# Joined moving operands, two-pass sums of squares for three head vectors, and a later scaling of the fox key

## The reference

```python
def hybrid_layer(h, ...):                       # first block
    u = rms_norm(h, mix_norm_g)
    p = u @ w_in                                # 2048 -> qkv_a, z, b, a, qkv_b, f, two gates
    y_a = gated_deltanet_branch(...)            # 16 heads of 128
    y_b = fox_branch(...)                       # 16 heads of 128
    mix = sigmoid(gate_a) * (y_a @ w_o_gdn) + sigmoid(gate_b) * (y_b @ w_o_fox)
    h = h + mix @ w_out
    u = rms_norm(h, mlp_norm_g)
    return h + square(relu(u @ w_up)) @ w_down

# what the change touches inside a head:
k  = k * rsqrt(sum(k * k) + eps)                # gated deltanet key, over 128
fq = fq * rsqrt(mean(fq * fq) + eps) * gain     # fox query
fk = fk * rsqrt(mean(fk * fk) + eps) * gain     # fox key
# in each chunk of 128 tokens: solve (I + strict_lower(beta k k^T decay)) w = rhs
```

## Time and profile before

| | us |
|---|---|
| median of 3 runs | 2772.41 |
| lowest and highest | 2772.25, 2773.69 |
| the profiled execution's own time | 2774.34 |
| its span | 2772.5 |
| PE busy in the span | 2740.4 (99%) |
| DVE, ACT, POOL busy | 2018.1, 1409.7, 290.1 |
| mix stage, about | 58 to 917 of the span |

### The profile page before, as it was taken

How to read it: one execution, slowest core, us unless ns; L and a number is a source line. 1 busy time by engine, 2 the same in 40 slices (tenths; PEclk the granted TensorE clock), 3 DMA queues, 4 the chain that set the end, 5 groups by cost and what they waited for, 6 DMA issues and landing times.

```text
span 2772.5 us, 50822 instructions
## 1 busy us (share of the span) xinstructions
PE 2740.4 (99%) x17645; PEld 2466.9 (89%) x17645; DVE 2018.1 (73%) x3665; ACT 1409.7 (51%) x2437; POOL 290.1 (10%) x259
## 2 busy tenths in 40 slices
PE   7999999999999999999999999999999999999998
PEld 7999999999999888888888888888888998888887
DVE  7887888788788666667765666756777777788875
ACT  6556655655665434444443444534545555445553
POOL 0000000000000000004700000000460001500024
PEclk9999999999999999999999999999999999999999
DMA  6444444444454555566565555665555554554445
GB/s 216 150 156 138 155 142 155 138 148 154 142 155 135 178 190 188 183 191 217 177 196 189 181 192 182 190 192 182 192 177 175 164 168 159 183 166 144 144 156 181
DMA packets 130235, 472.74 MB, mean 171 GB/s; under 512 B 15136, under 2 KB 15136, under 8 KB 129952
## 3 DMA queue, kind: packets, MB, share of 16 engines
q1 hardware_dynamic: 126144, 457.37, 51.3%
q0 software_dynamic: 3936, 13.34, 1.6%
HBM read 468.40 MB, written 2.25 MB: 170 GB/s over the span
## 4 chain that ended last, share of the span: by engine, by line
PE 95%; DVE 2%; ACT 1%; issue 1%; DMA 0%; DVEq 0%; SPq 0%; ACTq 0%
PE bank L310 42%; PE bank L311 21%; PE bank L312 7%; PE bank L313 7%; PE bank L314 7%; PE bank L808 1%; PE bank L854 1%; PE bank L863 1%; DVE w_lo L286 1%; PE bank L1078 1%; PE bank L1238 0%; PE bank L920 0%; PE bank L1155 0%; PE bank L1254 0%; PE bank L874 0%
## 5 line engine op out<-in xcount | busy, mean ns | idle before, releaser
L286 DVE TENSOR_TENSOR w_lo<-raw,w_hi 128x1024 fp32r<-128x1024 f32 x862 | 1058.7, 1253 | 133.5 <-ACT w_hi L280 129.2
L280 ACT ACTIVATE w_hi<-raw 128x1024 fp32r<-128x1024 f32 x862 | 896.9, 1053 | 438.6 <-PE bank L311 426.4
L310 PE MATMUL bank<-u,w_hi 128*128 128x512 f32 x2768 | 995.9, 401 | 0.0
L311 PE MATMUL bank<-u,w_lo 128*128 128x256 f32 x2768 | 779.0, 281 | 0.0
L310 PE MATMUL bank<-ya,w_hi 128*128 128x512 f32 x1792 | 629.7, 395 | 0.7 <-DVE h L2199 0.7
L310 PEld LDWEIGHTS bank<-u,w_hi 128*128 128x128 f32 x2768 | 520.5, 188 | 115.5 <-issue 2.8
L311 PEld LDWEIGHTS bank<-u,w_lo 128*128 128x128 f32 x2768 | 523.0, 189 | 0.9
L311 PE MATMUL bank<-ya,w_lo 128*128 128x256 f32 x1792 | 504.9, 282 | 0.0
L312 PE MATMUL bank<-u,w_hi 128*128 128x272 f32 (+2 forms) x1552 | 483.5, 312 | 4.9 <-DVE u L434 2.9
L313 PE MATMUL bank<-u,w_hi 128*128 128x272 f32 (+2 forms) x1552 | 445.3, 287 | 0.0
L314 PE MATMUL bank<-u,w_lo 128*128 128x272 f32 (+2 forms) x1552 | 445.1, 287 | 0.0
(11 more groups left out here) (401 smaller groups left out, 3140.3 us busy)
## 6 DMA issues: line engine op xcount, KB each, us to landing
raw<-in_stream SPq DMA_DIRECT2D x864, 512.0 KB, 3.7
mix_row<-rows POOLq DMA_DIRECT2D x16, 408.0 KB, 4.7
xT<-in_xT SPq DMA_DIRECT2D x4, 544.0 KB, 5.9
mix_coef_m<-meta_rows POOLq DMA_DIRECT2D x16, 128.0 KB, 4.5
h<-in_xT POOLq DMA_DIRECT2D x1, 2048.0 KB, 9.4
out_dram<-h SPq DMA_DIRECT2D x8, 256.0 KB, 2.4
consts<-in_consts POOLq DMA_DIRECT2D x1, 1817.0 KB, 8.2
meta_rows<-mix_b_mat POOLq DMA_DIRECT2D x16, 1.0 KB, 3.0
```

Of the source, the lines that this page charges most:

```text
L280: act.activation(w_hi[:, slot], raw[:, slot], ACT.Copy).then_inc(hi_ready, 1)
L286: dve.tensor_tensor(w_lo[:, slot], raw[:, slot], w_hi[:, slot].bitcast(F32), ALU.subtract).then_inc(lo_ready, 1)
L310: pe.matmul(o, a, x, start=first, stop=False)
L311: return pe.matmul(o[:, 0:SEQ], b, x[:, 0], start=False, stop=last)
```

## The change

Three things are changed.

The layout: `ya` becomes `[P, KT, 536]`, of which the first 512 elements are used, in one piece: part 0 and part 1 stand side by side, with 2144 bytes from one `k` to the next. A second name `ux` with the same layout is put on `u`'s place. From the MLP on, writers and readers of `u` use `ux` (up, the second block's projections and gates); the mix and merge stages still read `u` in the old layout. What lies behind `ya` moves by 512 bytes.

The sums: for the deltanet key, the fox query and the fox key, ScalarE squares twice, into a float32r tile `sq_hi` and into `sq`. VectorE writes the rest, `sq` minus `sq_hi`, over `sq` as float32r. TensorE multiplies both by float32r ones (`ones_r`), in two matmuls. The deltanet output's sum stays as it was. The new VectorE step stands at 70 (key), 90 (fox query) and 103 (fox key); the sums move from 80 to 81, from 96 to 98 and from 104 to 106, the transpose from 97 to 98, where it comes behind the sum.

The order: the fox key's scaling, `unit fk`, moves on VectorE from 105 to 108 and comes behind `level 1`.

```diff
+BLOCK = 2 * SEQ + 24
-        ya_at = region(2 * KT * TOK * 4)
-        ya_rows = place("ya", [P, KT, 2, TOK], F32R, ya_at)
-        ya_x = ya_rows[:, :, :, META:]
+        ya_at = region(KT * BLOCK * 4)
+        def joined(name, where):
+            both = place(name, [P, KT, BLOCK], F32R, where)[:, :, 0:2 * SEQ]
+            return both.rearrange("p k (a n) -> p k a n", a=2)
+        ya_x = joined("ya", ya_at)
+        ux = joined("ux", u_at)
+        ones_r = mt("ones_r", [P, P], F32R)
+        sq_lo = place("sq_lo", [P, TOK], F32R, mt.at["sq"])
+        sq_hi = {"gdn k": place("sq_hi_k", [P, TOK], F32R, mt.at["qk"])}
+        for x in ("fox q", "fox k"):
+            sq_hi[x] = place("sq_hi_" + x.replace(" ", "_"), [P, TOK], F32R, mt.at["th"])
+        SPLIT = ("gdn k", "fox q", "fox k",)
 # PE_PLAN
-            (28, "columns"), (80, "k sum"), ..., (96, "fq sum"), (97, "transpose"),
-            (101, "prod", 1), (104, "fk sum"), (107, "step", 1), ...
+            (28, "columns"), (81, "k sum"), ..., (98, "fq sum"), (98, "transpose"),
+            (101, "prod", 1), (106, "fk sum"), (107, "step", 1), ...
 # TensorE, ones_sum
+                if name in SPLIT:
+                    pe.wait_ge(sem("cleared"), 19)
+                    pe.matmul(bank[2][:, :width], ones_r[:], sq_hi[name][:, :width], start=True, stop=False)
+                    pe.matmul(bank[2][:, :width], ones_r[:], sq_lo[:, :width], start=False,
+                              stop=True).then_inc(sem("length sum"), 1)
+                    return
 # ScalarE, square
+                if name in SPLIT:
+                    act.activation(sq_hi[name][:, :width], src, ACT.Square, scale=pre)
+                    act.activation(sq[:, :width], src, ACT.Square, scale=pre).then_inc(sem("squared"), 1)
+                    return
 # VectorE
+            def dve_rest(name, n, width):
+                dve.wait_ge(sem("squared"), squares_of_head(name, n))
+                dve.tensor_tensor(sq_lo[:, :width], sq[:, :width], sq_hi[name][:, :width].bitcast(F32),
+                                  ALU.subtract).then_inc(sem("length sq"), 1)
 # readers, for example
-                matrix(f"up{q}", u_seq, ...)
+                matrix(f"up{q}", ux_seq, ...)
```

More of the change, by code:

```diff
@@ L236, in __init__ @@
             def __init__(self, tag, spans):
-                self.tag, self.spans = tag, [list(s) for s in spans]
+                self.tag, self.spans, self.at = tag, [list(s) for s in spans], {}
             def __call__(self, name, shape, dt=F32):
@@ L565, in program @@
         PE_PLAN = (
-            (28, "columns"), (80, "k sum"), (84, "turn"), (87, "qk"), (88, "kk"), (96, "fq sum"), (97, "transpose"),
-            (101, "prod", 1), (104, "fk sum"), (107, "step", 1), (110, "turn inverse", 1), (110, "prod", 2), (112, "step", 2),
+            (28, "columns"), (81, "k sum"), (84, "turn"), (87, "qk"), (88, "kk"), (98, "fq sum"), (98, "transpose"),
+            (101, "prod", 1), (106, "fk sum"), (107, "step", 1), (110, "turn inverse", 1), (110, "prod", 2), (112, "step", 2),
             (115, "turn inverse", 2), (115, "prod", 3), (116, "logits"), (116, "turn v"), (117, "step", 3), (124, "turn inverse", 3), (124, "prod", 4), (124, "turn p"),
@@ L579, in program @@
             (36, "conv", "v"), (49, "conv", "q"), (51, "silu", "v"), (60, "conv", "k"), (62, "silu", "q"),
[L580 to L582 removed]
+            (68, "silu", "k"), (70, "k rest"), (71, "unit k"), (72, "g diff"), (72, "fox bias"), (76, "silu", "z"), (84, "decay b"),
+            (86, "b mat"), (90, "fq rest"), (92, "qk"), (96, "level", 0), (98, "mask", 1), (99, "q dec"), (103, "unit fq"), (103, "fk rest"),
+            (108, "level", 1), (108, "unit fk"), (112, "inverse turned", 1), (112, "mask", 2), (112, "level", 2), (114, "inverse turned", 2), (114, "mask", 3),
             (114, "logits"), (119, "level", 3), (120, "soft"), (120, "inverse turned", 3), (120, "mask", 4), (127, "level", 4), (127, "meta", 0),
@@ L1054, in _ @@
             for q in range(QUARTERS):
[L1055 removed]
+                matrix(f"up{q}", ux_seq, ("u lo", KT, 1), None if q else lambda: total(pe, 0))
                 matrix(f"down{q}", ya, ("hidden lo", (q + 1) * KT, 1))
@@ L1067, in _ @@
             for t in range(MLA_IN_TILES):
-                full_tile(pe, "mla_in", t, u_seq, 2 * SEQ, 2 * t, ready=("u lo", 2 * KT, 1), midway=midways.get(t))
+                full_tile(pe, "mla_in", t, ux_seq, 2 * SEQ, 2 * t, ready=("u lo", 2 * KT, 1), midway=midways.get(t))
             LOGITS_BANK, TURNED_BANK = (bank[2], bank[7]), (bank[3], bank[4])
@@ L1208, in swa_products @@
                         for k in range(HALF_KT):
-                            mm = product(pe, slot, k, o, u_seq(half * HALF_KT + k), half == 0 and k == 0,
+                            mm = product(pe, slot, k, o, ux_seq(half * HALF_KT + k), half == 0 and k == 0,
                                          half == 1 and k == HALF_KT - 1)
@@ L1781, in _ @@
                 dve.memset(x[:], 0.0).then_inc(sem("cleared"), 1)
+            dve.tensor_copy(ones_r[:], const("ones")).then_inc(sem("cleared"), 1)
             dve.wait_ge(sem("sc act"), 4)
@@ L2057, in _ @@
                          "unit k": lambda n: unit("gdn k", n, kT, TOK, 0.5, "unit k"), "b mat": dve_b_mat,
-                         "o add": dve_o_add,
+                         "o add": dve_o_add, "k rest": lambda n: dve_rest("gdn k", n, TOK),
+                         "fq rest": lambda n: dve_rest("fox q", n, SEQ),
+                         "fk rest": lambda n: dve_rest("fox k", n, TOK),
                          "q dec": dve_q_dec, "qk": dve_qk, "level": dve_level, "inverse turned": dve_inverse_turned, "decay b": dve_decay_b, "mask": dve_mask,
```

22 lines of the change are left out of this document (14 added, 8 removed), and 2 rows, old and new, of the table ACT_PLAN.

## The result

The changed kernel takes 2790.99 us (median of 4 runs, 2790.28 to 2791.41), the kernel before on the same chip 2772.33 (4 runs). The ratio is 1.0066, with a 95% interval of 1.0053 to 1.0078: slower by 18.7 us, where 2789 was predicted. The profiled execution took 2791.01, its span is 2789.2. The spans of the two profiles differ by 16.7 and not by 18.7, because the profiled execution of the kernel before lies 1.9 above its median.

A forecast was written before the change was run, and what follows sets the result against it. TensorE was taken to bound the kernel, without slack at three waiting places of the mix. Mix +24 and layout -7 gave +17 us on 2774.3, 2791, stated as 2789 against the runs' median; range 2759 to 2807, leaving 2 in 10 out.

The forecast's parts named there:

- The bound: Whole kernel: TensorE busy almost everywhere; in the mix, anything added ahead of its three waiting places is paid by TensorE.
- The sums: Mix: two rounded passes replace each float32 sum, saving 0.20 us a sum, 9.6 us if nothing else is late.
- The key's chain: Mix, deltanet key: second square and rest bring scaled key and turn 0.6 us later; output steps charged nothing.
- The fox query's chain: Mix: rest behind the slab split, TensorE waits 1.4 us at the sum, first product later by 1.6 us per head.
- The fox key: Mix: even exchange at level 1; a wait of 0.2 us put against the 0.20 saved, so nothing.
- The mix: Mix stage: costs 1.5 us per head over 16 heads, +24 us; term limits -9.6 and +32.
- The layout: 3536 `ya` and `u` blocks: -2 ns each at 2144 bytes, -7 us; span -25 to +12.
- A: Rival, mix: the waits are covered, sums save 9.6 and layout 7 us, giving 2756; chance 0.18.
- B: Rival, layout: every joined block goes at 0.343 us, -25 + 24 = -1, giving 2772; chance 0.18.
- C: Rival, layout: joined blocks cost what `mx` shows, +12 + 24 = +36, giving 2808; chance 0.12.
- D: Rival, layout: it does nothing, as the address is not what matters; +24, giving 2796; chance 0.12.
- The range: Whole kernel: forecast's own range 2779 to 2801, from mix +18 to +28 and layout -16 to 0; chance 0.40.

The follow-up runs named there:

- fk_level2: Against the kernel before: joined layout, of the three sums only the fox key's in two passes, sum at 108, scaling behind level 2; 2762.99 us, ratio 0.9964.
- both_fox: Against `fk_level2`: fox query also in two passes, rests and scalings in gaps of VectorE's list, both roots behind ScalarE's slab of 104; 2767.03 us, 0.9978 to before.
- fq_whole: Changed kernel with the fox query's sum as before (one square, no rest, float32 sum at 96); 2778.63 us, ratio 1.0022 to the kernel before.
- fq_early: Changed kernel with VectorE's rest of the fox query at 86, ahead of the slab split, instead of 90; 2783.67 us, ratio 1.0039 to the kernel before.
- joined_2176: Kernel before with `ya` and `ux` joined, keeping 2176 bytes between blocks; 2767.96 us, ratio 0.9982.
- joined_2048: Kernel before with `ya` and `ux` joined, 2048 bytes between blocks; 2770.39 us, ratio 1.0003.
- layout: Kernel before with the joined layout alone (`ya` and `ux`, 2144 bytes between blocks), sums and order as before; 2766.08 us, ratio 0.9975.
- fox_behind: Against the kernel before: joined layout, fox query and fox key in two passes, rests behind levels 0 and 1, roots and scalings later; 2826.29 us, ratio 1.0193.

## Why the prediction was right

**The bound.** It stands as predicted: PE is busy nearly throughout, and what came into VectorE's and ScalarE's chain ahead of the key's turn and of the first product was paid by TensorE.

**The sums.** 0.43 to 0.45 for float32 and 0.24 to 0.25 for two rounded passes were right; `fk_level2` shows the 0.20 per head when nothing else is late. What failed is the lower bound of the term, -9.6 for three sums: the query's sum is worth nothing where it stands, for VectorE sets the first product (`both_fox`), and for the key the rest and second square cost more than they save. Only the fox key's -3 was had, and only with a later sum and scaling.

**The key's chain.** Turn later by 0.6, waits of about 0.4 and 0.7 were predicted; measured are 0.54 over the stretch, 0.49 and 0.67, and taking the key out gives 8.6 us back. The output steps cost nothing, as said.

**The fox query's chain.** Its order was right: rest behind the slab split, the product later by 1.6 in all, of which 0.6 are the key's. Measured are 0.54 + 1.03 = 1.57. The wait came out longer, 1.69 where 1.4 was predicted, and the delay did not. I deducted the float32 sum from TensorE's way to block 98, and forgot that the transpose had left it too: two blocks of 0.38 and it had taken 1.05, so it is worth 0.29. TensorE came sooner by that and waited longer for the same rest, which changes no delay. From the sum to the product it then took 1.57 (457.10 to 458.67), where 1.47 had been summed, with 0.1 for the transpose.

**The fox key.** 0 was predicted and 0.02 measured, and the wait of 0.2 against the 0.20 saved was met (0.19). That it came out so is luck: the wait was put there without a row, and it was this short only because the wait of the query stood ahead of it. Without that one it was 0.40, and the key cost 0.24 per head (`fq_whole` and `fq_early`).

**The mix.** +24 predicted, 16 x 1.58 = 25.3 by the heads, 25.7 from its first block to the first of merge, of which 23.8 lie from the second head on.

**The layout.** -7 us predicted, -6.4 measured alone. -2 ns a block was near (-2.5 in up and down), but that was in part luck, for it was chosen between two rows, and the step "joined is not by itself faster, what decides is the address" is wrong, as `joined_2176` shows. I had read it from `mx` and `yb` at 353 and 352, and that is one of two paces that this form has: in `joined_2048` it goes at 352.9 in merge and at 346.7 in up and down, and `mx` itself goes at 346.7 in most of the out stage of `fq_whole`. What decides between them stays open.

The rule of 16 byte lines of the Trainium skill ("SBUF — State Buffer", "Specifications (TRN2)"), by which all these layouts would be equal, is not borne out: they all read whole lines, and differ by up to 3.3 ns a block in up and down.

**The rivals.** A (waits covered, 2756) was refuted as it stood, with 37.1 and 10.6 us of waits. B (343 ns a block) falls: no long stretch of `ya`, `u` or `mx` blocks went faster than about 346.5. It was read from one distance (0.34), and a single one is no pace: behind that first `yb` block the distances in the trace are 350, 361 and 349 ns in turn, 353.3 in the mean. C (joined as `mx`) is real for 2048 in merge, and not for 2144. D (layout nothing) falls by the interval of `layout`.

**The range.** The forecast's own range, 2779 to 2801, does not follow from its terms: a mix of +18 and a layout of -16 give 2774, and only the upper end, +28 and 0, is 2800. The measured 2791 lies inside either.

## What to carry to other kernels

Before a step is made cheaper, ask who sets the next meeting of the two engines. Here 0.43 us of TensorE's time ahead of a wait for VectorE was free, and one instruction added to VectorE, the engine that was waited for, cost its full distance of 0.34 at the better of two places ahead of that meeting; at the other the stretch grew by 1.03. An instruction that must wait (a scaling for its Exp, a root for its sum) belongs behind the steps that others need, also on an engine that is half idle. And a wait found to cost little may be shortened by another: measure it again when that one is gone.

## What the hardware showed that was not expected

Blocks of one form and one count of columns (512 and 256) took 350.0, 348.75, 348.33, 347.5 or 346.67 ns in the mean of undisturbed stretches of up and down, by the layout of the moving operand. At the upper level of the clock, 2.4 GHz, these are 840, 837, 836, 834 and 832 cycles, whole numbers each, and 353.3 is 848. With 2048 bytes between blocks the pace changed between 346.7 and 353 from stage to stage at unchanged addresses, and for `mx` inside a stage in three traces, and the runs of `joined_2048` fell into two kinds 11 to 15 us apart; with 2144 neither merge nor up and down was at 353 in any of the eleven traces that have it.

In `fox_behind` the idle time of one wait (PE busy 0.73 and 1.40 of two stretches of 2 us) was followed by a granted clock of 0.55 and 0.59, and so it was in 11 of 16 heads with such a wait. In the changed kernel, whose waits are shorter (1.9 at the longest), the mix stands at 1.00.
